# Two steps of a token mixer moved: the additions of a dilated attention block ahead of its filler, and the rounding of stick-breaking weights to another engine

## The chip, the cores and the metric

One core of a Trainium2 chip runs the kernel. The metric is the device time of one execution, in microseconds (us). Of the kernel before there are three timed runs: 1128.93, 1130.28 and 1131.22 us, with the median at 1130.28 us. The profile is of one further execution.

## What is computed

One decoder layer over 512 tokens of width 1024, in float32: a half-step SwiGLU FFN, a token-mixing sub-layer, a second half-step FFN, and an RMSNorm. The mixer reads one normalised input through one projection and runs two attentions on it. The stick-breaking one has 8 heads:

```python
strict = s_pos < t_pos
log_not = jnp.where(strict, jax.nn.log_sigmoid(-z), 0.0)
between = lax.cumsum(log_not, axis=3, reverse=True) - log_not
a = jnp.where(strict, jnp.exp(jax.nn.log_sigmoid(z) + between), 0.0)
outs.append(jnp.einsum('bhqk,bhkd->bhqd', a.astype(vb.dtype), vb))
```

The dilated one has 4 slots of keys and values and three groups of queries; the softmax groups of one slot are mixed by their denominators. Both outputs are projected, gated by sigmoids of the input, added, and projected once more.

## The kernel before

**Arithmetic.** TensorE multiplies at float32r, a rounded form of float32. To keep the precision each operand is held as a rounded high part and the rest as a low part, and a product is three matmuls (`product`, lines 1209 to 1211). So every weight tile of 128 x 1024 that a DMA brings costs one rounding copy on ScalarE (`split_hi`, line 489) and one subtraction on VectorE (`split_lo`, line 791), and every activation tile is split in the same way. ScalarE makes most high parts, VectorE all low parts. The tile `spA_hi` is an exception: VectorE rounds it too.

**Order.** Every engine runs its own queue in program order, and semaphores hold it at each hand-over. In the mixer all three compute engines follow one hand-written list, `MIX_STEPS` (made by `mix_schedule`, lines 106 to 168). Its fillers are half units of the projection (`Ua`, `Ub`, or `Us` for a short unit): 12 matmuls on TensorE each, while `Ua` and `Us` also carry the split of the weight tile two units later on ScalarE and VectorE. The fillers stand between the steps of the attentions, so that TensorE has matmuls to do while ScalarE and VectorE work on a head or a block.

**Stick-breaking heads 0 to 7** (about 380 to 530 us). `scores` makes the logits in three parts (512, 256 and 512 columns); ScalarE takes abs, exp and ln (lines 692 to 696), VectorE adds the maximum and splits the result (1098 to 1105). `suffix` sums it on TensorE with triangular matrices (1416, 1417); ScalarE takes the exponential of the three parts into `ebuf` (702), VectorE rounds each part into `spA_hi` (1113) and subtracts for `spA_lo` (1115). `pv` multiplies them by the values (1217, 1219). Between these stand the fillers, the rotation of the rotary projections (four ScalarE copies, line 648, then VectorE lines 1075 and 1080, then the split 683 and 1085) and the split of the outputs (716 and 1126).

**Dilated blocks 0 to 15** (about 525 to 665 us). Block n is slot n // 4 and quarter n % 4 of the queries. `dscores` makes the logits in `pair_bank`; VectorE takes the row maximum (1140) and its negative (1142), ScalarE the exponential with its sum into `prob` (730). `dadd` is the part that the change moves: VectorE takes the reciprocal of the sum (1151) and makes two additions (1155), and ScalarE multiplies `prob` by the reciprocal (736). `dturn` transposes `prob` on TensorE (1456) and ScalarE copies the rounded result to `pT_hi` (744); `dlo` subtracts on VectorE for `pT_lo` (1163). The `dscores` of the next block waits for the exponential, since `pair_bank` is single. Each `fill` here adds one filler. Before, one block stands in the list as:

```python
fill(DL_FILL[n] - 1)
...
s.append(("dadd", (j, r)))
if n + 1 < len(blocks):
    s.append(("dscores", blocks[n + 1]))
fill(1)
...
s.append(("dturn", (j, r)))
s.append(("dlo", (j, r)))
```

In blocks 0 to 3 the fillers and the `fin` steps behind them still carry rotary projections, which put the rotation (648) and its split on ScalarE and VectorE within each block; later blocks have gates in their place.

Of the kernel before, what the change touches and what calls it, by code (L numbers as in the profile page):

```python
# [78 lines left out]
SB_WIDTH = (512, 256, 512)  # L79
SB_AT = (0, 512, 768)  # L80
# [28 lines left out]
def mix_schedule():  # L109


    s = []
    halves = [(half, u) for u in range(MIX, END)
              for half in (("Us",) if u >= GATE and (u - GATE) % 2 else ("Ua", "Ub"))]

    def fill(n):
        for _ in range(n):
            half, u = halves.pop(0)
            s.append((half, u))

            if MIX < u <= GATE and half == ("Ub" if MIX_ORDER[u - 1 - MIX][0] in ("rq", "rk") else "Ua"):
                s.append(("fin", u - 1))
            if half == "Ub" and u >= GATE:
                s.append(("gate", u))
            if half == "Us":
                s.append(("merge", u))

    fill(2)
    s.append(("norm", 1))
    fill(4)  # L130
    s.append(("scores", 0))
    for h in range(2 * SB_PAIRS):
        fill(SB_FILL[h][0])
        if h:
            s.append(("y", h - 1))
        s.append(("suffix", h))
        if h:
            s.append(("ysplit", h - 1))
        fill(SB_FILL[h][1])
        s.append(("scores", h + 1) if h + 1 < 2 * SB_PAIRS else ("dscores", (0, 0)))  # L140
        s.append(("pv", h))
    blocks = [(j, r) for j in range(2 * DL_PAIRS) for r in range(DIL)]
    for n, (j, r) in enumerate(blocks):
        fill(DL_FILL[n] - 1)
        if n == 0:
            s.append(("y", 2 * SB_PAIRS - 1))
        if n == 1:
            s.append(("ysplit", 2 * SB_PAIRS - 1))
        s.append(("dadd", (j, r)))
        if n + 1 < len(blocks):  # L150
            s.append(("dscores", blocks[n + 1]))
        fill(1)
        if r == 0 and j:
            s.append(("dpv", j - 1))
        s.append(("dturn", (j, r)))
        s.append(("dlo", (j, r)))
        if r == 0 and j:
            s.append(("dy", j - 1))
        if r == 1 and j:
            s.append(("dysplit", j - 1))  # L160
    fill(len(halves))
    s.append(("dpv", 2 * DL_PAIRS - 1))
    s.append(("dy", 2 * DL_PAIRS - 1))
    s.append(("dysplit", 2 * DL_PAIRS - 1))
    return s
# [22 lines left out]
def build(nc, A, out):  # L188
    F32, F32R, BF16 = mybir.dt.float32, mybir.dt.float32r, mybir.dt.bfloat16
    ALU, ACT, AX = mybir.AluOpType, mybir.ActivationFunctionType, mybir.AxisListType  # L190
    ctx = ExitStack()
    with ctx:
# [56 lines left out]
        with ExitStack() as mix:  # L249
# [5 lines left out]
            with ExitStack() as att:  # L255
                raw = sb("raw", [P, 2, SEQ], F32, att)
                with ExitStack() as s:
                    spA_hi = sb("spA_hi", [P, 1280], F32R, s)
                    spA_lo = sb("spA_lo", [P, 1280], F32R, s)
                    ebuf = sb("ebuf", [P, 1280], F32, s)  # L260
# [94 lines left out]
        a_done = sem("a_done")  # L355
# [127 lines left out]
        def _(act):  # L483
# [153 lines left out]
            for kind, w in MIX_STEPS:  # L637
# [59 lines left out]
                elif kind == "suffix":  # L697
                    if w == 2 * SB_PAIRS - 1:
                        act.preload_act_table_set("exp_and_others")
                    for b in range(3):  # L700
                        act.wait_ge(suffix_done, 3 * w + b + 1)
                        act.activation(ebuf[:, SB_AT[b]:SB_AT[b] + SB_WIDTH[b]], bank[b][:, 0:SB_WIDTH[b]],
                                       ACT.Exp).then_inc(a_done, 1)
                elif kind in ("y", "dy"):

                    rows, other = head_rows(w), head_rows(w + 1)
                    n = w + (2 * SB_PAIRS if kind == "dy" else 0)
                    act.wait_ge(pv_done, n + 1)
                    if n >= 2:
                        act.wait_ge(ys_done, n - 1)  # L710
                    act.activation(ysum[rows, :], bank[3][other, :], ACT.Copy).then_inc(y_cross_done, 1)
                elif kind in ("ysplit", "dysplit"):
                    rows = head_rows(w)
                    if kind == "ysplit":
                        act.wait_ge(y_whole, w + 1)
                        act.activation(ys_hi[rows, w // 2, :], ysum[rows, :], ACT.Copy).then_inc(ys_hi_done, 1)
                    else:

                        act.wait_ge(y_whole, 2 * SB_PAIRS + w + 1)
                        act.activation(yd_hi[rows, w // 2, :].rearrange("c (p r) -> c r p", r=DIL),  # L720
                                       ysum[rows, :].rearrange("c (r p) -> c r p", r=DIL),
                                       ACT.Copy).then_inc(ys_hi_done, 1)
                elif kind == "dscores":
                    n = DIL * w[0] + w[1]
                    act.wait_ge(max_step, 2 * (n + 1))
                    if n >= 2:
                        act.wait_ge(pt_turned, n - 1)
                    if n == 0:
                        act.wait_ge(pv_done, 2 * SB_PAIRS)
                    act.activation(prob[:, n % 2, :], pair_bank[:, 0:6 * P], ACT.Exp,  # L730
                                   bias=stats[:, n % 2, 1:2], scale=HD ** -0.5,
                                   accum_out=stats[:, n % 2, 2:3]).then_inc(p_done, 1)
                elif kind == "dadd":
                    n = DIL * w[0] + w[1]
                    act.wait_ge(p_step, 3 * n + 3)
                    act.activation(prob[:, n % 2, 0:SEQ], prob[:, n % 2, 0:SEQ], ACT.Copy,
                                   scale=stats[:, n % 2, 3:4]).then_inc(p_scaled, 1)
                elif kind == "dturn":
                    j, r = w
                    n = DIL * j + r  # L740
                    act.wait_ge(pt_turned, n + 1)
                    if r == 0 and j:
                        act.wait_ge(pv_done, 2 * SB_PAIRS + j)
                    act.activation(pT_hi[:, :, r * P:(r + 1) * P], bank[2].rearrange("p (b c) -> p b c", b=DIL),
                                   ACT.Copy).then_inc(pt_hi_done, 1)
# [39 lines left out]
        def _(dve):  # L785
# [250 lines left out]
            for kind, w in MIX_STEPS:  # L1036
# [70 lines left out]
                elif kind == "suffix":  # L1107
                    for b in range(3):
                        t = 3 * w + b
                        cols = slice(SB_AT[b], SB_AT[b] + SB_WIDTH[b])  # L1110
                        dve.wait_ge(a_done, t + 1)
                        dve.wait_ge(suffix_done, 3 * w + 3)
                        dve.tensor_copy(spA_hi[:, cols], ebuf[:, cols]).then_inc(a_hi_done, 1)
                        dve.wait_ge(a_hi_done, t + 1)
                        dve.tensor_tensor(spA_lo[:, cols], ebuf[:, cols], spA_hi[:, cols].bitcast(F32),
                                          ALU.subtract).then_inc(a_split, 1)
# [450 lines left out]
```

## Time and profile before

| | |
|---|---|
| median of the three runs | 1130.28 us |
| profiled execution, its own time | 1132.13 us |
| its span | 1130.3 us |
| TensorE busy | 1106.8 us (98%) |
| VectorE busy | 769.8 us (68%) |
| ScalarE busy | 543.2 us (48%) |
| mean granted TensorE clock | 0.992 |

The profiled execution's own time is 1.8 us over its span and 1.9 us over the median of the runs. The profile names engines PE (TensorE), DVE (VectorE), ACT (ScalarE), POOL (GpSimd) and SP (the DMA queue). A timeline row gives the start and the duration in us, the engine, the line, the operation with its output and inputs, and in brackets the idle time of the engine before it with what ended it. An instruction may start before the one ahead of it has ended, by some tenths of a us; a row's `x4` stands for four instructions in a row.

### The profile page before, as it was taken

To read this page: it belongs to the slowest core of one execution; us is meant where nothing else is said; L and a number is where in the kernel's file an instruction comes from. 1 tells how busy PE (TensorE), PEld (TensorE's weight loads), DVE (VectorE), ACT (ScalarE), POOL (GpSimd) and SP (SyncE) were. 2 spreads that over 40 slices of the span, in tenths; PEclk is the share of its full clock that TensorE was granted. 3 is DMA by queue.
4 is the path that set the end of the run, shared out by engine and by line. 5 is a ranking of instruction groups with operands and counts; after the bars stand their busy time and mean duration, and the time that the engine had idled before them with its cause. 6 is when DMAs were issued, how large, how long until landed. Compare 5 with 4: busy or idle time off the path is not lost.

```text
span 1130.3 us, 15634 instructions
## 1 busy us (share of the span) xinstructions
PE 1106.8 (98%) x6057; PEld 948.1 (84%) x6065; DVE 769.8 (68%) x1074; ACT 543.2 (48%) x870; POOL 2.7 (0%) x6
## 2 busy tenths in 40 slices
PE   8999999999999999999999999999999999999996
PEld 6888899988998788877777778788898899889985
DVE  6876378745878778678765556667774588637863
ACT  6554155533653456567654443425452355415541
POOL 0000000000000000000000000000000000000000
PEclk9999999999999999999999999999999999999997
DMA  8223233333324212111121113422233323323222
GB/s 288 94 75 112 74 113 112 113 93 93 103 71 126 75 39 75 57 56 47 38 67 65 52 54 97 143 93 94 96 103 101 104 84 112 96 92 112 93 57 75
DMA packets 34440, 102.99 MB, mean 91 GB/s; under 512 B 4160, under 2 KB 7616, under 8 KB 34368
## 3 DMA queue, kind: packets, MB, share of 16 engines
q1 hardware_dynamic: 34368, 102.01, 28.3%
q8 instruction: 47, 0.77, 0.3%
q14 instruction: 25, 0.20, 0.1%
HBM read 99.90 MB, written 2.10 MB: 90 GB/s over the span
## 4 chain that ended last, share of the span: by engine, by line
PE 88%; DVE 4%; ACT 3%; issue 2%; SPq 1%; DMA 1%; POOL 0%; POOLq 0%; DVEq 0%; ACTq 0%
PE acc_pair L1209 25%; PE acc_pair L1211 25%; PE acc_pair L1210 25%; PE pair_bank L1209 2%; PE pair_bank L1211 2%; PE pair_bank L1210 2%; PE bank L1209 1%; PE bank L1211 1%; PE bank L1210 1%; ACT rope L648 1%; DVE w_lo L791 1%; ACT w_hi L489 1%; PE bank L1217 1%; PE bank L1219 1%; DMA w_raw<-in_w13a 1%
## 5 line engine op out<-in xcount | busy, mean ns | idle before, releaser
L1209 PE MATMUL acc_pair<-xg_hi,w_hi 128*128 128x512 f32 (+1 forms) x693 | 265.8, 384 | 1.7 <-DVE w_lo L1022 1.7
L1210 PE MATMUL acc_pair<-xg_lo,w_hi 128*128 128x512 f32 (+1 forms) x693 | 260.2, 375 | 0.0
L1211 PE MATMUL acc_pair<-xg_hi,w_lo 128*128 128x512 f32 (+1 forms) x693 | 259.4, 374 | 0.0
L489 ACT ACTIVATE w_hi<-w_raw 128x1024 fp32r<-128x1024 f32 (+3 forms) x159 | 154.4, 976 | 147.6 <-PE acc_pair L1211 147.3
L791 DVE TENSOR_TENSOR w_lo<-w_raw,w_hi 128x1024 fp32r<-128x1024 f32 (+3 forms) x159 | 178.6, 1126 | 42.9 <-ACT w_hi L489 37.5
L1211 PEld LDWEIGHTS acc_pair<-xg_hi,w_lo 128*128 128x128 f32 x693 | 130.7, 189 | 24.5
L1209 PEld LDWEIGHTS acc_pair<-xg_hi,w_hi 128*128 128x128 f32 x693 | 131.1, 189 | 23.9 <-issue 2.9
L1210 PEld LDWEIGHTS acc_pair<-xg_lo,w_hi 128*128 128x128 f32 x693 | 131.3, 189 | 20.3 <-issue 1.0
L1211 PE MATMUL acc_pair<-hid_hi,w_lo 128*128 128x512 f32 x352 | 138.8, 394 | 0.0
L1210 PE MATMUL acc_pair<-hid_lo,w_hi 128*128 128x512 f32 x352 | 138.2, 393 | 0.0
L1209 PE MATMUL acc_pair<-hid_hi,w_hi 128*128 128x512 f32 x352 | 136.9, 389 | 0.0
L962 DVE SCALAR_TENSOR_TENSOR x<-acc_pair,x 128x512 f32<-128x512 f32 x56 | 38.7, 691 | 113.8 <-PE acc_pair L1211 113.6
L1210 PEld LDWEIGHTS acc_pair<-hid_lo,w_hi 128*128 128x128 f32 x352 | 66.1, 188 | 15.0
L1209 PEld LDWEIGHTS acc_pair<-hid_hi,w_hi 128*128 128x128 f32 x352 | 66.1, 188 | 14.5
L1211 PEld LDWEIGHTS acc_pair<-hid_hi,w_lo 128*128 128x128 f32 x352 | 66.2, 188 | 13.4
L521 ACT ACTIVATE s_hi<-s_raw 128x1536 fp32r<-128x1536 f32 x35 | 52.1, 1488 | 47.5 <-DVE s_raw L863 47.5
L878 DVE TENSOR_TENSOR s_lo<-s_raw,s_hi 128x1536 fp32r<-128x1536 f32 x35 | 61.5, 1758 | 13.7 <-ACT s_hi L521 13.7
L890 DVE TENSOR_TENSOR acc_pair<-acc_pair,ysum 128x512 f32<-128x512 f32 x35 | 24.5, 700 | 56.1 <-PE acc_pair L1211 56.1
L1209 PE MATMUL acc_pair<-t_hi,s_hi 128*128 128x256 f32 x210 | 59.5, 283 | 2.6 <-ACT acc_pair L573 2.6
L1211 PE MATMUL acc_pair<-t_hi,s_lo 128*128 128x256 f32 x210 | 59.4, 283 | 0.0
L1210 PE MATMUL acc_pair<-t_lo,s_hi 128*128 128x256 f32 x210 | 59.3, 282 | 0.0
L536 ACT ACTIVATE gate<-gate 128x512 f32<-128x512 f32 x44 | 27.6, 627 | 49.6 <-DVE gate L892 49.6
(223 smaller groups left out, 2072.7 us busy)
## 6 DMA issues: line engine op xcount, KB each, us to landing
w_raw<-in_w13b SPq DMA_DIRECT2D x44, 512.0 KB, 3.6
w_raw<-in_w13a SPq DMA_DIRECT2D x40, 512.0 KB, 3.6
w_raw<-in_wmix SPq DMA_DIRECT2D x22, 512.0 KB, 3.5
w_raw<-in_w2a SPq DMA_DIRECT2D x16, 512.0 KB, 3.5
w_raw<-in_w2b SPq DMA_DIRECT2D x16, 512.0 KB, 3.6
w_raw<-in_wgate SPq DMA_DIRECT2D x8, 512.0 KB, 3.5
w_raw<-in_wend SPq DMA_DIRECT2D x8, 512.0 KB, 3.4
w_raw<-in_wo SPq DMA_DIRECT2D x8, 512.0 KB, 3.4
```

Source lines behind the costliest of these rows:

```text
L489: act.activation(w_hi[:, s, 0:width], w_raw[:, s, 0:width], ACT.Copy).then_inc(whi_done, 1)
L521: act.activation(s_hi[:, g % 2], s_raw[:], ACT.Copy).then_inc(s_hi_done, 1)
L536: act.activation(gate[:, f % 2, :], gate[:, f % 2, :], ACT.Silu).then_inc(silu_done, 1)
L648: act.activation(rope2[to:to + HD // 2, t % 2, :].rearrange("c (r p) -> c r p", r=DIL), acc[w % RING][c:c + HD // 2, :].rearrange("c (p r) ...
L791: dve.tensor_tensor(w_lo[:, s, 0:width], w_raw[:, s, 0:width], w_hi[:, s, 0:width].bitcast(F32), ALU.subtract).then_inc(wlo_done, 1)
L878: dve.tensor_tensor(s_lo[:, g % 2], s_raw[:], s_hi[:, g % 2].bitcast(F32), ALU.subtract).then_inc(s_lo_done, 1)
L890: dve.tensor_tensor(late, late, p5, ALU.add).then_inc(p5_added, 1)
L962: dve.scalar_tensor_tensor(x[:, m, :], acc[s][:], scale, x[:, m, :], ALU.mult, ALU.add).then_inc(acc_read[s], 1)
L1209: pe.matmul(o, w_h, r_h, start=first, stop=False, skip_group_check=check)
L1210: pe.matmul(o, w_h, r_l, start=False, stop=False, skip_group_check=check)
L1211: return pe.matmul(o, w_l, r_h, start=False, stop=last, skip_group_check=check)
L1217: pe.matmul(bank[3][:, col:SEQ], v[:, P * a:P * (a + 1)], a_h, start=first, stop=False, skip_group_check=True)
```

## The change

Two edits. The step `dadd` of every block moves ahead of the first filler of the block. And the three roundings of `ebuf` into `spA_hi` of each head leave VectorE; ScalarE does them behind the three exponentials, as activations with the function Copy, and VectorE's subtractions wait for them. VectorE's wait for the exponentials goes, since the copies stand behind those.

```diff
     for n, (j, r) in enumerate(blocks):
+        s.append(("dadd", (j, r)))
         fill(DL_FILL[n] - 1)
         if n == 0:
             s.append(("y", 2 * SB_PAIRS - 1))
         if n == 1:
             s.append(("ysplit", 2 * SB_PAIRS - 1))
-        s.append(("dadd", (j, r)))
         if n + 1 < len(blocks):
             s.append(("dscores", blocks[n + 1]))
         fill(1)
@@ scalar, kind == "suffix"
                         act.activation(ebuf[:, SB_AT[b]:SB_AT[b] + SB_WIDTH[b]], bank[b][:, 0:SB_WIDTH[b]],
                                        ACT.Exp).then_inc(a_done, 1)
+                    for b in range(3):
+                        cols = slice(SB_AT[b], SB_AT[b] + SB_WIDTH[b])
+                        act.wait_ge(a_done, 3 * w + b + 1)
+                        act.activation(spA_hi[:, cols], ebuf[:, cols], ACT.Copy).then_inc(a_hi_done, 1)
@@ vector, kind == "suffix"
                         cols = slice(SB_AT[b], SB_AT[b] + SB_WIDTH[b])
-                        dve.wait_ge(a_done, t + 1)
                         dve.wait_ge(suffix_done, 3 * w + 3)
-                        dve.tensor_copy(spA_hi[:, cols], ebuf[:, cols]).then_inc(a_hi_done, 1)
                         dve.wait_ge(a_hi_done, t + 1)
                         dve.tensor_tensor(spA_lo[:, cols], ebuf[:, cols], spA_hi[:, cols].bitcast(F32),
                                           ALU.subtract).then_inc(a_split, 1)
```

Lines of the changed kernel behind the edits are 4 higher on ScalarE and on VectorE up to the removed ones, and 2 higher after them. TensorE's order is the same in both.

ScalarE's queue at the `suffix` and `ysplit` steps of a head, up to the next weight split; before:

```order
L702 ACTIVATE ebuf<-pair_bank 128x512
L702 ACTIVATE ebuf<-pair_bank 128x256
L702 ACTIVATE ebuf<-bank 128x512
L716 ACTIVATE ys_hi<-ysum 64x512
L489 ACTIVATE w_hi<-w_raw 128x1024
```

and with the change:

```order
L702 ACTIVATE ebuf<-pair_bank 128x512
L702 ACTIVATE ebuf<-pair_bank 128x256
L702 ACTIVATE ebuf<-bank 128x512
L707 ACTIVATE spA_hi<-ebuf 128x512
L707 ACTIVATE spA_hi<-ebuf 128x256
L707 ACTIVATE spA_hi<-ebuf 128x512
L720 ACTIVATE ys_hi<-ysum 64x512
L489 ACTIVATE w_hi<-w_raw 128x1024
```

Three copies into `spA_hi` stand between the last exponential (702) and the split of the output, `ys_hi`, and the next weight split, `w_hi`.

VectorE's queue from `dlo` of block 1 to the row maximum of block 3; before:

```order
L1163 TENSOR_TENSOR pT_lo<-bank,pT_hi 128x4x128
L791 TENSOR_TENSOR w_lo<-w_raw,w_hi 128x1024
L1151 RECIPROCAL stats<-stats 128x1
L1155 TENSOR_TENSOR prob<-prob 128x128 x2
L1140 TENSOR_REDUCE stats<-pair_bank 128x1
```

and with the change:

```order
L1165 TENSOR_TENSOR pT_lo<-bank,pT_hi 128x4x128
L1153 RECIPROCAL stats<-stats 128x1
L1157 TENSOR_TENSOR prob<-prob 128x128 x2
L795 TENSOR_TENSOR w_lo<-w_raw,w_hi 128x1024
L1142 TENSOR_REDUCE stats<-pair_bank 128x1
```

The reciprocal and the additions for block 2 stand ahead of the weight split `w_lo` now, directly behind `pT_lo` of block 1.

ScalarE's queue at the same place, from the exponential of block 2 (L730, with the change L734) to that of block 3; before:

```order
L730 ACTIVATE prob,stats<-pair_bank,stats 128x768
L648 ACTIVATE rope<-acc_pair 32x512 x4
L683 ACTIVATE dq_hi<-roped 128x512
L744 ACTIVATE pT_hi<-bank 128x4x128
L489 ACTIVATE w_hi<-w_raw 128x1024
L736 ACTIVATE prob<-prob,stats 128x512
L730 ACTIVATE prob,stats<-pair_bank,stats 128x768
```

and with the change:

```order
L734 ACTIVATE prob,stats<-pair_bank,stats 128x768
L648 ACTIVATE rope<-acc_pair 32x512 x4
L683 ACTIVATE dq_hi<-roped 128x512
L748 ACTIVATE pT_hi<-bank 128x4x128
L740 ACTIVATE prob<-prob,stats 128x512
L489 ACTIVATE w_hi<-w_raw 128x1024
L734 ACTIVATE prob,stats<-pair_bank,stats 128x768
```

The scaling of block 2 (`prob<-prob,stats`) stands ahead of the weight split `w_hi` now, behind `pT_hi` of block 1.

## Rows read from the trace of the kernel before

**Rows 1.** The page: the span, and the busy time of the engines.

```profile
span 1130.3 us, 15634 instructions
...
PE 1106.8 (98%) x6057; PEld 948.1 (84%) x6065; DVE 769.8 (68%) x1074; ACT 543.2 (48%) x870; POOL 2.7 (0%) x6
```

**Rows 2.** Waits of TensorE: who released it, us in total, times, longest.

```profile
PE bank L1456 <- ACT prob L736: 1.6, 2, 1.1
...
PE pair_bank L1416 <- DVE spA_lo L1105: 1.4, 1, 1.4
...
PE bank L1217 <- DVE sv L1089: 0.5, 1, 0.5
```

**Rows 3.** Timeline of VectorE, 455 to 520: start, duration, operation.

```profile
473.41 0.43 DVE L1113 CAST spA_hi<-ebuf 128x512 fp32r<-128x512 f32 x1
...
475.59 0.69 DVE L1115 TENSOR_TENSOR spA_lo<-ebuf,spA_hi 128x512 fp32r<-128x512 f32 x1
...
491.12 0.41 DVE L1113 CAST spA_hi<-ebuf 128x512 fp32r<-128x512 f32 x1
...
493.30 0.69 DVE L1115 TENSOR_TENSOR spA_lo<-ebuf,spA_hi 128x512 fp32r<-128x512 f32 x1
```

**Rows 4.** Timeline of ScalarE, 455 to 530.

```profile
472.79 0.61 ACT L702 ACTIVATE ebuf<-bank 128x512 f32<-128x512 f32 x1
...
485.48 0.61 ACT L683 ACTIVATE sq_hi<-raw 128x512 fp32r<-128x512 f32 x1
...
490.94 0.60 ACT L702 ACTIVATE ebuf<-bank 128x512 f32<-128x512 f32 x1
...
527.48 2.43 ACT L648 ACTIVATE rope<-acc_pair 32x512 f32<-32x512 f32 x4 [2.88 <-DVE raw L1002]
```

**Rows 5.** Timeline of VectorE, 516 to 572.

```profile
550.39 0.68 DVE L1163 TENSOR_TENSOR pT_lo<-bank,pT_hi 128x512 fp32r<-128x512 f32 x1
...
551.28 1.23 DVE L791 TENSOR_TENSOR w_lo<-w_raw,w_hi 128x1024 fp32r<-128x1024 f32 x1 [0.21 <-ACT w_hi L489]
...
552.49 0.60 DVE L1155 TENSOR_TENSOR prob<-prob 128x128 f32<-128x128 f32 x2
...
553.01 0.95 DVE L1140 TENSOR_REDUCE stats<-pair_bank 128x1 f32<-128x768 f32 x1
```

**Rows 6.** Timeline of ScalarE, 516 to 572.

```profile
540.24 0.60 ACT L744 ACTIVATE pT_hi<-bank 128x512 fp32r<-128x512 f32 x1
...
545.57 0.90 ACT L730 ACTIVATE prob<-pair_bank,stats 128x768 f32<-128x768 f32 x1 [0.34 <-DVE stats L1142]
...
546.59 2.43 ACT L648 ACTIVATE rope<-acc_pair 32x512 f32<-32x512 f32 x4
...
549.70 0.60 ACT L744 ACTIVATE pT_hi<-bank 128x512 fp32r<-128x512 f32 x1
...
550.19 1.05 ACT L489 ACTIVATE w_hi<-w_raw 128x1024 fp32r<-128x1024 f32 x1
...
553.13 0.72 ACT L736 ACTIVATE prob<-prob,stats 128x512 f32<-128x512 f32 x1 [1.88 <-DVE prob L1155]
...
554.18 0.90 ACT L730 ACTIVATE prob<-pair_bank,stats 128x768 f32<-128x768 f32 x1 [0.33 <-DVE stats L1142]
...
558.31 0.60 ACT L744 ACTIVATE pT_hi<-bank 128x512 fp32r<-128x512 f32 x1
```

**Rows 7.** Timeline of TensorE, 540 to 575.

```profile
545.29 0.66 PE L1456 MATMUL bank<-identf,prob 128*128 128x128 f32 x4 [1.08 <-ACT prob L736]
...
548.64 0.50 PE L1209 MATMUL pair_bank<-dk_hi,dq_hi 64*128 64x512 f32 x1
...
553.90 0.66 PE L1456 MATMUL bank<-identf,prob 128*128 128x128 f32 x4 [0.47 <-ACT prob L736]
...
557.26 0.49 PE L1209 MATMUL pair_bank<-dk_hi,dq_hi 64*128 64x512 f32 x1
...
561.84 0.60 PE L1456 MATMUL bank<-identf,prob 128*128 128x128 f32 x4
```

## Prediction

> **What bounds the kernel now.** I read the page first: TensorE is busy for 1106.8 of the 1130.3 us of the span [rows 1], so only the remaining 23.5 us can be won by moving work between the other engines, and most of those lie at the start and the end of the program, which the change does not touch. Then I read the waits of TensorE. In the part that is touched they come to little: 1.6 us in two waits of a transposition (line 1456) for the scaling of `prob`, 1.4 us in one wait of the sums (1416) for `spA_lo`, and 0.5 us before one product with the values (1217) [rows 2]. So both edits together can win at most some 3.5 us. What they can lose is not bounded that way. So I read the timelines of VectorE and ScalarE around these waits, to see how late the two run behind TensorE and what sets their pace.
>
> **Edit 1, the rounding of the weights.** It takes 24 casts from VectorE: 16 of 512 columns at 0.41 to 0.43 us [rows 3] and 8 of 256 columns, shorter ones. It gives ScalarE 24 copies. A rounding copy of 512 columns from SBUF takes 0.61 us there [rows 4], and the next instruction can start some 0.1 us before it ends (`pT_hi` from 549.70 for 0.60 us, the next from 550.19 [rows 6]). What counts is when the last subtraction of a head ends, since behind it VectorE goes on to the work that TensorE will ask for.
>
> In head 4 VectorE casts first at 473.41 and starts its last subtraction at 475.59 [rows 3]. The last exponential on ScalarE starts at 472.79 [rows 4]. With the change the three copies start behind it at about 473.3, 473.8 and 474.15, and the last ends at 474.8; the three subtractions follow each copy by 0.04 us, and the last one starts at about 474.9, so 0.65 us sooner. In head 5 VectorE casts from 491.12 and subtracts last at 493.30 [rows 3]. There the last exponential starts at 490.94 [rows 4], pulled forward by the 0.65 us of head 4; the same count gives a last subtraction at 492.25, 1.05 us sooner. In head 6 the gain is small, because the weight split on ScalarE now stands behind three copies, and in head 7 it is nothing. With what is handed on through VectorE's unbroken queue, the first rotation ahead of the dilated blocks, at 527.48 [rows 4], comes 1.2 us sooner. For TensorE I take 1.1 us of the 1.4 us wait and a quarter of a us of the 0.5 us wait [rows 2]: 1.35 us, as long as nothing later takes it back. For heads 0 to 3 TensorE has no wait for this work; the copies' 1.5 us of ScalarE are hidden there by its idle times, and I put them at zero (if that cover were gone, 0.4 us in head 3, where ScalarE is busiest). Bounds for this edit: from 0 to 1.9 us sooner.
>
> The Trainium skill, "ScalarE: Activation LUTs", section "Rules for kernel authors", asks for a budget of about 0.3 us per activation and 0.83 ns per element. By that a copy of 512 columns would be estimated at 0.72 us, the trace has 0.61 us [rows 4], and three copies in a row would take about 0.6 us more per head than I count; over heads 4 and 5 the relief would be gone. What that makes of the time is the first rival.
>
> **Edit 2, the additions ahead of the filler.** TensorE waits for the scaling of blocks 1 and 2, 1.08 us and 0.47 us [rows 7]. The edit puts the additions, and ScalarE's scaling, ahead of the weight split of the filler. This brings the scaling forward, but by more waiting between the engines, and everything behind it comes later. Block 2 of before: `pT_hi` of block 1 starts on ScalarE at 549.70, the weight split `w_hi` follows at 550.19 [rows 6] while VectorE makes `pT_lo` (550.39), then `w_lo` at 551.28, the additions at 552.49 and the row maximum of block 3 at 553.01 [rows 5]. That is 3.3 us from `pT_hi` to the maximum.
>
> With the change the same work is a chain: `pT_lo` ends 1.4 us after the start of `pT_hi`; additions 0.60 us [rows 5], to 2.0 us; scaling 0.72 us [rows 6], of which 0.1 us overlaps with the next, to 2.65; `w_hi` 1.05 us, to 3.7; `w_lo` 1.23 us, and the maximum at about 4.9 us. So the maximum, and with it the exponential (554.18 before [rows 6]), the rotation of 2.43 us, the split and `pT_hi` of the next block come 1.6 us later per block. This is a closed loop: from one `pT_hi` to the next it took 8.61 us (549.70 to 558.31) [rows 6], more than TensorE's own 7.94 us from 553.90 to 561.84 [rows 7]. It was the loop, not TensorE, that set the pace of blocks 1 and 2. It becomes 10.2 us.
>
> I follow `pT_hi` of block 2, at 558.31 before [rows 6]. It comes 1.2 us sooner by edit 1; 0.25 us later by block 0, where most of the added chain is absorbed by a wait that was there; 1.4 us later by block 1 (540.24 to 549.70, 9.46 us before [rows 6], 10.85 now); 1.6 us later by block 2. That puts it at 560.35. The scaling of block 3 ends 2.75 us behind it, at 563.1, and TensorE's transposition of block 3, at 561.84 before without a wait [rows 7], starts at 563.15: 1.3 us later.
>
> The waits show the same. The 1.08 us of block 1 go. But `dscores` of block 3, which ran at 548.64, needs the exponential that started at 545.57, and `dscores` of block 4 (557.26) the one that started at 554.18 [rows 6, 7]; each now waits about 0.85 us. The transpositions of blocks 2 and 3 wait about 1.1 and 1.3 us. From block 3 on the rotation leaves the loop. ScalarE and VectorE are 4 to 6 us later than before by then and win it back over blocks 4 to 7, during which TensorE reaches them with under 0.5 us to spare; for this I add 0.45 us (none to 1). After that the shift stays as it is, since the rest of the program is TensorE's. DMA is no part of this: the weight splits are later by 2 to 5 us, while a tile is split about two units ahead of its use.
>
> **Sum.** 1.3 + 0.45 = 1.75 us later than the profiled execution, so 1133.9 us against its own 1132.13 us. That execution lies 1.9 us over the median; against the median of 1130.28 us the same shift gives **1132.0 us**. With 0 to 1.9 us for edit 1, 0.2 us per pass of the loop either way and the tail's bounds, this case runs from 1130.5 to 1133.5 us.
>
> **The rivals.**
>
> *No relief from edit 1* (chance 0.2). If the copies on ScalarE cost 0.7 us each and don't overlap, heads 4 and 5 end where they did. For it speaks that ScalarE holds back weight splits too, which VectorE then waits for; against it that a rounding copy takes 0.61 us [rows 4] and that the next one overlaps with it [rows 6]. Then the 1.2 us are missing from the loop's start: 2.95 us later, 1133.2 us, from 1132.5 to 1134.5 us.
>
> *Faster* (chance 0.13). The mechanism is slack in the loop of blocks 1 and 2: if the scaling runs in ScalarE's idle 1.88 us [rows 6] and the weight split still reaches the row maximum in time, the two waits of 1.55 us [rows 7] go and the 1.35 us of the heads stay, together 2.9 us, 1127.4 us; with half of it 1128.8 us. It decides from the point at which the maximum comes less than 0.5 us later per block; I count 1.6 us. Against it speaks that every step of the new chain has an instruction that waits for the one before it.
>
> *They cancel* (chance 0.17). The relief of the heads and the waits of the blocks come out equal, because block 1 absorbs more than I count, or TensorE's arrival at block 3 has some slack: 1129.8 to 1130.8 us, at 1130.3 us.
>
> **How the numbers follow.** The forecast has a chance of 0.5. A measurement of this kernel tells a difference of about 0.2%, 2.26 us, from none. Of the forecast's range only the upper part is slower by more than that, a third of it (0.17), and of the first rival nearly all (0.2): 0.37. Of the faster case about half passes the bound: 0.07. The rest, 0.56, is within 0.2%. The range from 1129.0 to 1134.3 us takes in the forecast, most of the first rival and the upper part of the faster one.
>
> **What would show it right or wrong.** In the changed kernel's waits of TensorE: no wait of the transposition of block 1; new waits of line 1209 into `pair_bank` for the exponential (line 734), about 0.85 us each, at `dscores` of blocks 3 and 4; waits of 1.1 and 1.3 us for the scaling (740) at blocks 2 and 3; the wait for `spA_lo` down from 1.4 to 0.3 us. In ScalarE's timeline: 24 copies of line 707 at about 0.6 us for the wide ones, and 10.2 us between `pT_hi` of blocks 1 and 2. It would be wrong if that distance stays under 9.2 us, if the copies take over 0.7 us, or if waits appear in the later blocks, which I count as TensorE's.

## The result, and the profile after

The changed kernel takes 1135.80 us (median of six runs, 1132.80 to 1137.44), and the kernel before 1130.62 us (six runs, 1128.93 to 1131.22). The ratio is 1.0045 with an interval of 1.0031 to 1.0060. So it is slower by 5.2 us, where 1.75 us was forecast, and lies outside the range of 1129.0 to 1134.3 us. The sign of the sum was right. Its size was not.

The page of the changed kernel, in the same two places as [rows 1]; this execution's own time is 1137.42 us:

```profile
span 1135.6 us, 15634 instructions
...
PE 1109.8 (98%) x6057; PEld 949.9 (84%) x6065; DVE 760.3 (67%) x1050; ACT 552.8 (49%) x894; POOL 2.7 (0%) x6
```

VectorE gave up 9.5 us of work and ScalarE took 9.6 us on. That moves no bound: TensorE is busy for 98% as before, and its own busy time is 3.0 us longer, although it has the same matmuls. This last number is worth a stop: a wait leaves the matmuls behind it almost as they were (four transpositions take 0.66 us behind a wait and 0.60 us without one, [rows 7]), so a few waits don't make 3 us of busy time. It will come back as the clock.

The waits of TensorE from 380 to 680 us in the changed kernel (engine, tile and line, what ended the wait: us in total, times, longest), against [rows 2]:

```profile
PE pair_bank L1211 <- ACT prob L734: 2.3, 2, 1.4
PE bank L1458 <- ACT prob L740: 2.0, 2, 1.0
PE bank L1219 <- issue: 1.9, 1, 1.9
...
PE pair_bank L1418 <- DVE spA_lo L1109: 0.6, 1, 0.6
PE bank L1219 <- DVE sv L1093: 0.4, 1, 0.4
```

Two waits of `dscores` for an exponential (first line) are new, 2.3 us. The transpositions still wait twice, now 2.0 us for 1.6. The wait for `spA_lo` fell from 1.4 to 0.6 us. The third line is the product of the last block with `dv`; before it was 1.5 us, in a group that the prediction did not use (`issue` stands where the profile shows nothing that ended the wait):

```profile
PE bank L1217 <- issue: 1.5, 1, 1.5
```

Where the new waits lie is seen in TensorE's timeline (start, duration, and in brackets the idle time before). These are `dscores` of block 3, the transposition of block 2, `dscores` of block 4 and the transposition of block 3; that of block 1 starts at 544.65 without a wait.

```profile
549.36 0.46 PE L1211 MATMUL pair_bank<-dk_hi,dq_hi 64*128 64x512 f32 x1 [1.35 <-ACT prob L734]
...
555.11 0.66 PE L1458 MATMUL bank<-identf,prob 128*128 128x128 f32 x4 [1.02 <-ACT prob L740]
...
559.49 0.46 PE L1211 MATMUL pair_bank<-dk_hi,dq_hi 64*128 64x512 f32 x1 [0.97 <-ACT prob L734]
...
565.24 0.33 PE L1458 MATMUL bank<-identf,prob 128*128 128x128 f32 x1 [0.99 <-ACT prob L740]
```

ScalarE's timeline through two passes of the loop, to be laid beside [rows 6]:

```profile
541.36 0.60 ACT L748 ACTIVATE pT_hi<-bank 128x512 fp32r<-128x512 f32 x1
...
552.34 0.60 ACT L748 ACTIVATE pT_hi<-bank 128x512 fp32r<-128x512 f32 x1
554.34 0.72 ACT L740 ACTIVATE prob<-prob,stats 128x512 f32<-128x512 f32 x1 [1.39 <-DVE prob L1157]
554.96 1.04 ACT L489 ACTIVATE w_hi<-w_raw 128x1024 fp32r<-128x1024 f32 x1
558.35 0.90 ACT L734 ACTIVATE prob<-pair_bank,stats 128x768 f32<-128x768 f32 x1 [2.35 <-DVE stats L1144]
...
562.47 0.60 ACT L748 ACTIVATE pT_hi<-bank 128x512 fp32r<-128x512 f32 x1
```

and VectorE's in the same pass, beside [rows 5]:

```profile
553.03 0.68 DVE L1165 TENSOR_TENSOR pT_lo<-bank,pT_hi 128x512 fp32r<-128x512 f32 x1
...
553.70 0.60 DVE L1157 TENSOR_TENSOR prob<-prob 128x128 f32<-128x128 f32 x2
556.04 1.23 DVE L795 TENSOR_TENSOR w_lo<-w_raw,w_hi 128x1024 fp32r<-128x1024 f32 x1 [1.74 <-ACT w_hi L489]
557.18 0.95 DVE L1142 TENSOR_REDUCE stats<-pair_bank 128x1 f32<-128x768 f32 x1
```

Read the brackets as a relay. ScalarE stands 1.39 us for the additions, and has not yet made `w_hi`. VectorE then stands 1.74 us for `w_hi`, and so the row maximum starts 4.84 us behind `pT_hi` (557.18 less 552.34), where it was 3.31 us. Each engine idles in turn for the other. From `pT_hi` of block 1 to that of block 2 it takes 10.13 us for 8.61 us.

**The account of the two profiled executions.** I set marks at TensorE's starts that both traces have, and compare the distance between them:

| stretch | before | after | difference |
|---|---|---|---|
| scores of head 1 to values product of head 6 | 114.89 | 114.05 | -0.84 |
| values product of head 6 to `dscores` of block 0 | 10.11 | 11.61 | +1.50 |
| `dscores` of block 0 to the transposition of block 3 | 36.23 | 39.02 | +2.79 |
| transposition of block 3 to the last block's product | 100.81 | 101.49 | +0.68 |
| last block's product to the start of the projection behind the mixer | 56.95 | 58.55 | +1.6 |

These make +5.7 us of the span's +5.3; the rest of the program is 0.4 us shorter. The first, third and fourth rows are waits, +2.6 us together. The second and fifth are none. There TensorE's clock is lower. (Of the fourth, 0.2 us is no wait either: it falls in the few matmuls right behind the first mark.) Its windows in the changed kernel (stretch, length, busy time and instructions, granted clock, DMA share, GB/s):

```profile
510.00:515.00 5.00, 4.58 (x23) 0.95 0.08 7
515.00:520.00 5.00, 5.00 (x20) 0.71 0.26 97
...
665.00:670.00 5.00, 3.27 (x11) 0.81 0.09 26
670.00:675.00 5.00, 5.00 (x20) 0.85 0.00 0
```

### The profile page after: what moved, and what is told of

It is laid out like the page before. It is cut to its first block, busy times and chain, and to the rows that moved or that the text cites. A ratio compares the mean times of both kernels' runs of the same rounds, so it can differ in the third digit from the quotient of the medians.

```text
span 1135.6 us, 15634 instructions
## 1 busy us (share of the span) xinstructions
PE 1109.8 (98%) x6057; PEld 949.9 (84%) x6065; DVE 760.3 (67%) x1050; ACT 552.8 (49%) x894; POOL 2.7 (0%) x6
## 4 chain that ended last, share of the span: by engine, by line
PE 86%; DVE 5%; ACT 4%; issue 3%; SPq 1%; DMA 1%; POOL 0%; POOLq 0%; DVEq 0%; ACTq 0%
PE acc_pair L1211 24%; PE acc_pair L1212 24%; PE acc_pair L1213 24%; PE pair_bank L1211 2%; PE pair_bank L1213 2%; PE pair_bank L1212 2%; ACT rope L648 1%; PE bank L1211 1%; PE bank L1213 1%; PE bank L1212 1%; ACT w_hi L489 1%; PE bank L1219 1%; PE bank L1221 1%; DVE w_lo L795 1%; DMA w_raw<-in_w13a 1%
```

## The experiments

Two theories were set against each other. **The loop** (L): the change lengthens the closed loop of blocks 0 to 3, and what it costs is the waits shown. **The clock** (C): part of the loss comes from stretches at the lower of TensorE's two levels, which the loop doesn't explain. Each experiment has a profiled trace, from which the same marks are read, and timed runs beside the kernel before. The numbers of all stand in one table behind the last of them.

**One edit at a time.** The additions alone:

```diff
     for n, (j, r) in enumerate(blocks):
+        s.append(("dadd", (j, r)))
         fill(DL_FILL[n] - 1)
...
-        s.append(("dadd", (j, r)))
```

> Edit 2 alone: the additions and the scaling ahead of the first filler in all blocks; VectorE keeps rounding the weights. Theory L (the loop): the time is lost because the scaling stands ahead of the weight split on ScalarE, which makes the loop from one pT_hi to the next 10.1 us in blocks 1 and 2 (8.6 us before). In the changed kernel's trace the rotation ahead of block 0 was 0.70 us later than before and the transposition of block 3 3.40 us later, so blocks 0 to 3 cost 2.7 us; with 0.2 us in the blocks behind and 0.5 us at the last product, L expects 3.4 us more than before, new waits for the exponential (line 730) of 0.9 to 1.4 us at dscores of blocks 3 and 4, and full clock from 500 to 530 us. Rival C (the clock): the blocks cost nothing net, and what was lost is TensorE at its lower clock after waits, some 1.5 us in each such stretch; C expects under 1 us more than before where no such stretch shows, and 1.5 us for each that does.

Measured: 1134.66 us, ratio 1.0044 (1.0031 to 1.0057). Blocks 0 to 3 take 38.95 us, +2.72 against before, as in the changed kernel, and the waits are the same ones:

```profile
PE pair_bank L1209 <- ACT prob L730: 2.2, 2, 1.3
PE bank L1456 <- ACT prob L736: 2.0, 2, 1.0
PE bank L1217 <- issue: 2.0, 1, 2.0
PE pair_bank L1416 <- DVE spA_lo L1105: 1.4, 1, 1.4
```

The loss belongs to this edit. The wait for `spA_lo` stays at 1.4 us, as it must without the other.

The rounding alone (the diff is the scalar and vector part of the change, and no part of the list):

> Edit 1 alone: ScalarE rounds the weights, the additions stay behind the filler. Both theories take the relief of the heads from the changed kernel's trace: the product at 515.50 us before starts 0.9 us sooner. L expects 0.9 us less than before if the clock stays up, with the loop of blocks 1 and 2 at 8.6 us and the waits for the scaling as before. C expects a stretch of the lower clock from 514.6 to 517.6 us again, which belongs to this edit, and so 0.6 us more than before, with the loop at 8.6 us.

Measured: 1130.34 us, ratio 0.9993 (0.9981 to 1.0005), not to be told from before. By the marks the heads are 0.87 us shorter, and blocks 0 to 3 take 36.21 us, unchanged. So the relief is there, but it is under a us, and nothing takes it back.

**Which blocks.** The additions ahead of the filler in blocks 4 to 15 only:

```diff
     for n, (j, r) in enumerate(blocks):
+        if n >= 4:
+            s.append(("dadd", (j, r)))
         fill(DL_FILL[n] - 1)
...
-        s.append(("dadd", (j, r)))
+        if n < 4:
+            s.append(("dadd", (j, r)))
```

> Both edits, but the additions stand ahead of the filler only in blocks 4 to 15, whose fillers carry no rotation; blocks 0 to 3 have them behind it as before. L expects the loss of 2.7 us in blocks 0 to 3 to be gone, the loop of blocks 1 and 2 at 8.6 us, no new wait for the exponential, and at most 0.5 us left at the last product: 0.4 us less than before at full clock. If instead the blocks from 4 on carry a cost of their own, it shows here as waits after 570 us and more than 1 us over before.

Measured: 1133.83 us, 1.0035 (1.0022 to 1.0048), in five runs. The trace says the opposite of the time: blocks 0 to 3 are back at 36.23 us and only the last product waits longer (1.9 us for 1.5), so at the same clock this kernel would be 0.37 us faster than before. Its profiled run indeed took 1129.82 us; the four others took 1133.7 to 1135.0 us, at granted clocks that average lower. This is the first sign of lost time that no wait shows, and it was not what the loop theory wants. The clock is the candidate, no more. It was run again:

> e3 again, unaltered: its first trace is 0.4 us faster than before between the marks, its timed runs are slower by a ratio of 1.0035 with a mean granted clock of 0.992 against 0.9945 of before. If that was a matter of the executions drawn, the ratio falls to about 0.9997 with a mean clock near 0.9945. If the order of the late blocks brings the clock down, the ratio stays above 1.002 and the mean clock below 0.993, and this trace shows where.

Measured: 1132.53 us, 1.0010 (0.9999 to 1.0021), twelve runs, mean 1131.97 us, with the same marks. A milder result than the first, on the same side, but its interval doesn't exclude that nothing changed.

The additions ahead in blocks 0 to 3 only (the same diff, with `n < 4` and `n >= 4` exchanged):

> Both edits, with the additions ahead of the filler in blocks 0 to 3 only, the counterpart of e3. L expects the whole 2.8 us of blocks 0 to 3 here, new waits for the exponential at dscores of blocks 3 and 4, 0.85 us less in the heads, and the last product's wait at 1.5 us: 2.1 us over before at full clock. If the loss came from the many late blocks, it is within 0.5 us of before.

Measured: 1134.08 us, 1.0032 (1.0018 to 1.0047). Blocks 0 to 3 take 39.04 us, and the last product waits 1.5 us as before. The whole loss of 2.8 us in waits of the blocks needs only these four.

And the late blocks without the rounding on ScalarE:

> The additions ahead of the filler in blocks 4 to 15 alone, without edit 1: heads and blocks 0 to 3 as before, at most 0.5 us more at the last product. At full clock 0.5 us over before. If the late blocks bring the clock down, it is 2 us or more over before with a mean clock below 0.993; if not, between 0 and 1 us over.

Measured: 1132.65 us, 1.0024 (1.0010 to 1.0039), while the marks give only +0.5 us. The late blocks thus come with lost time that no wait in the traces shows, with either placing of the rounding.

**The scaling left where it was.** If the loop is long because ScalarE stands for the additions ahead of its weight split, then VectorE's additions can go ahead while ScalarE's scaling stays behind. The list gets a step of its own for the scaling:

```diff
     for n, (j, r) in enumerate(blocks):
+        s.append(("dadd", (j, r)))
         fill(DL_FILL[n] - 1)
...
-        s.append(("dadd", (j, r)))
+        s.append(("dscale", (j, r)))
...
-                elif kind == "dadd":
+                elif kind == "dscale":
```

The last two lines are in ScalarE's function; the rounding is on ScalarE as in the change.

> Both edits, with edit 2 only on VectorE: the reciprocal and the additions stand ahead of the first filler, while ScalarE's scaling stays behind the weight split of the filler, where it was. By L the loss comes from the scaling in front of the weight split: here the split runs beside pT_lo and the additions again, and from pT_hi to the row maximum I count 0.6 us for pT_hi to its copy's end, 0.7 pT_lo, 0.6 additions and 1.2 w_lo, 3.1 us against 3.3 us before and 4.9 us with the change. So the loop is about 8.4 us, the scaling is ready 1.3 us sooner than before, and the waits of 1.08 and 0.47 us go: 1.5 to 2.5 us less than before at full clock. If the cost lies in the additions on VectorE themselves, this kernel is as slow as the changed one, 3 us or more over before.

Measured: 1129.38 us, 0.9992 (0.9979 to 1.0004). Blocks 0 to 3 take 34.86 us: 1.37 us less than before, 4.16 us less than with the change. Of the four waits of the change one is left:

```profile
PE bank L1459 <- ACT prob L741: 0.2, 1, 0.2
```

ScalarE's timeline of this kernel, block 2:

```profile
547.64 0.60 ACT L749 ACTIVATE pT_hi<-bank 128x512 fp32r<-128x512 f32 x1
548.14 1.05 ACT L490 ACTIVATE w_hi<-w_raw 128x1024 fp32r<-128x1024 f32 x1
549.63 0.72 ACT L741 ACTIVATE prob<-prob,stats 128x512 f32<-128x512 f32 x1 [0.44 <-DVE prob L1158]
551.83 0.90 ACT L735 ACTIVATE prob<-pair_bank,stats 128x768 f32<-128x768 f32 x1 [1.47 <-DVE stats L1145]
```

and VectorE's:

```profile
549.00 0.60 DVE L1158 TENSOR_TENSOR prob<-prob 128x128 f32<-128x128 f32 x2
549.52 1.22 DVE L796 TENSOR_TENSOR w_lo<-w_raw,w_hi 128x1024 fp32r<-128x1024 f32 x1
550.65 0.95 DVE L1143 TENSOR_REDUCE stats<-pair_bank 128x1 f32<-128x768 f32 x1
```

`w_hi` now runs beside `pT_lo` and the additions. VectorE finds it ready and stands nowhere, and the maximum starts 3.01 us behind `pT_hi`. The scaling, which is what TensorE waits for, starts 1.99 us behind `pT_hi`, where it was 3.43 us before [rows 6] and 2.00 us with the change. So the scaling comes as early as in the change, and the weight split doesn't pay for it.

The same order with the rounding left on VectorE:

> The order of e4 (additions ahead of the filler on VectorE, scaling behind the weight split on ScalarE) without edit 1. L expects blocks 0 to 3 to take 1.4 us less than before, as in e4, since the loop is shorter whatever the rounding, and the heads to take as long as before: 1.3 us less than before at full clock, against 2.1 us less for e4. If the gain of e4 came only from its earlier start into the blocks, this kernel shows under 0.5 us.

Measured: 1129.90 us, 0.9995 (0.9984 to 1.0006), blocks 0 to 3 in 34.85 us. The gain of the blocks doesn't need the other edit. In time it is not shown to be faster than before.

The first of the two once more, since it was the best:

> e4 again, unaltered, for a narrower interval: 2.1 us less than before at full clock (heads 0.85, blocks 0 to 3 1.4 us), which with the mean clock of its first runs (0.9936 against 0.9945) leaves about 1 us; a ratio of 0.998 to 0.9995.

Measured: 1128.09 us, twelve runs, 0.9979 (0.9966 to 0.9993). It beats before by about 2 us and the change by more than 6; the run before it left zero just inside its interval, so this is a small gain, clear of zero in one of two measurements.

**The wait of the last product.** In the changed kernel's trace the wait of 1.94 us before the last product is followed by a stretch at the lower level. Blocks 14 and 15 in the old order (`n < 14` ahead, `n >= 14` behind):

> Both edits, but in blocks 14 and 15 the additions stay behind the filler. TensorE's wait ahead of the last product, 1.94 us with the change and 1.46 us before, should be about 1.5 us again, which wins 0.4 us at full clock. The kernel with late blocks only (e3) is 0.4 us faster than before by its trace but 3.5 us slower in its timed runs. If the longer wait at the last product is what brings the lower clock at 668 us (C), this kernel is faster than the changed one by 0.4 us and up to 1.5 us more; if not, by 0.4 us alone, about 1135.4 us.

Measured: 1135.44 us, 1.0040 (1.0026 to 1.0055). The wait is back at 1.5 us and the time is no better. So taking the longer wait away did not win the time back. Whether it changes how often the clock falls, six executions can't tell: their mean clock is 0.9937, and that is uncertain by 0.001.

**The pair again**, to have the clock of more executions:

> The changed kernel again, unaltered, for a second trace. Between marks of the two traces, the changed kernel at full clock should cost 2.6 us more than before: 0.85 us less up to the product of head 6, 2.8 us more in blocks 0 to 3, 0.7 us more from there to the last product. By L these three parts repeat within 0.2 us in this trace. By C the stretches of the lower clock (385, 515 and 668 us in the first trace, about 1.5 us each) belong to the change and stand at the same places again; if they are a matter of the single execution, at least one of them is missing here, and the run is shorter by 1.5 us for each.

> The kernel before again, for a second trace: same marks within 0.2 us at full clock. In the first trace one stretch of the lower clock cost time (385 us). If such stretches fall by the single execution, this trace can have another number of them, at 385, 515 or 668 us, and the span moves by 1.5 us for each; if they belong to the kernel, only the one at 385 us shows.

Measured: the change 1134.68 us, 1.0042 (1.0027 to 1.0057), with marks as in its first trace (blocks 0 to 3 in 39.04 us) and neither of the two low stretches behind the heads. Before: 1130.24 us, 1.0003 (0.9990 to 1.0017).

**All of them, by waits and by clock.** The column "waits" is the difference from before in the marks' three waiting stretches, from one trace each, less what a low stretch adds where one falls into them (0.9 us in the trace of the last kernel, the only such case). The column "clock at most" is what a lower mean clock would take if TensorE had work in every us of the span: 1133 us times the difference of the mean granted clocks, where 83 executions of before have 0.9943 (mean time 1130.56 us). It is an upper bound, as is shown below the table.

| kernel | runs | waits, us | mean clock | clock at most, us | sum | mean time less before |
|---|---|---|---|---|---|---|
| before again | 10 | 0.0 | 0.9951 | -1.0 | -1.0 | -0.4 |
| change | 6 | +2.6 | 0.9927 | +1.8 | +4.4 | +5.1 |
| change again | 8 | +2.6 | 0.9925 | +2.0 | +4.6 | +4.4 |
| additions alone | 5 | +3.5 | 0.9940 | +0.3 | +3.8 | +4.5 |
| rounding alone | 12 | -0.9 | 0.9949 | -0.8 | -1.6 | -0.6 |
| late blocks | 5 | -0.4 | 0.9918 | +2.8 | +2.4 | +2.9 |
| late blocks again | 12 | -0.4 | 0.9928 | +1.7 | +1.3 | +1.4 |
| late blocks, rounding on VectorE | 12 | +0.5 | 0.9927 | +1.8 | +2.3 | +2.8 |
| early blocks | 12 | +2.2 | 0.9931 | +1.3 | +3.5 | +3.8 |
| last two blocks behind | 6 | +2.3 | 0.9937 | +0.7 | +3.0 | +4.5 |
| scaling behind | 11 | -2.1 | 0.9936 | +0.7 | -1.4 | -1.1 |
| scaling behind again | 12 | -2.1 | 0.9945 | -0.3 | -2.4 | -1.9 |
| scaling behind, rounding on VectorE | 12 | -1.3 | 0.9952 | -1.1 | -2.4 | -0.5 |

The mean times are uncertain by 0.4 to 0.9 us each. With that, ten of the twelve sums of changed kernels meet the time within 1.1 us; the kernel with the last two blocks behind misses by 1.5 and the last row by 1.9 us. Against the 25 executions of before that ran beside these two (0.9950, 1130.24 us) they miss by 1.0 and 1.5 us. But eleven of the twelve sums are too small, so something of about half a us is in none of the columns.

The clock's price in the table is too high, and the executions say by how much. Among the 83 of before, all of one kernel, the time rises by 0.63 us (standard error 0.04) for each 0.001 of mean clock, and within the sets of the other kernels by 0.74 us; the table takes 1.13 us. The trace of before shows why. TensorE's clock is low from 1118.60 us to the end in it, and that is more than half of the whole shortfall (5.9 of 9.3 us), but there TensorE has little to run and then nothing:

```profile
1110.00:1118.00 8.00, 7.34 (x39) 1.00 0.00 1
1118.00:1124.00 6.00, 4.41 (x22) 0.55 0.16 58
1124.00:1130.00 6.00, 0.00 (x0) 0.50 0.78 291
```

At 0.63 us the clock takes 1.1 us of the change (0.9926 over its fourteen executions), not 1.9 us, and then all twelve sums are too small, by 0.3 to 1.8 us.

## Why the prediction was wrong in size

**The loop, foreseen and there.** The distance between two `pT_hi` was put at 10.2 us; it is 10.13 us. From `pT_hi` of block 0 to that of block 1 it was put at 10.85 us; it is 10.98 us (541.36 to 552.34). The maximum was put at about 4.9 us behind `pT_hi`; it is 4.84 us. The prediction had `dscores` of block 0 start 1.35 us sooner and the transposition of block 3 start 1.3 us later, so the stretch between was 2.65 us longer; measured it is 2.79 us. So the mechanism was right, and two slips in it are small: block 0 adds 0.4 us behind the first rotation where 0.25 us was said, and block 1 adds 1.5 us where 1.4 us was said. No wait is left at block 1, as said. The single waits are distributed otherwise: 1.35 and 0.97 us at `dscores` of blocks 3 and 4 (0.85 each was said), 1.02 and 0.99 us at the transpositions of blocks 2 and 3 (1.1 and 1.3 said).

**First step that failed: the relief of the heads, 1.35 us.** VectorE's part came as counted in head 4 and nearly in head 5: the last subtraction ends at 475.62 us for 476.28 before (0.66 us sooner, 0.65 said) and at 493.13 for 493.99 (0.86, where 1.05 was said). The rows, of the copies of head 4 on ScalarE and of the subtractions of head 4 on VectorE:

```profile
473.24 1.47 ACT L707 ACTIVATE spA_hi<-ebuf 128x512 fp32r<-128x512 f32 x3
```

```profile
473.99 1.63 DVE L1117 TENSOR_TENSOR spA_lo<-ebuf,spA_hi 128x512 fp32r<-128x512 f32 x3 [0.63 <-ACT spA_hi L707]
```

Three copies, of 512, 256 and 512 columns, take 1.47 us together, so the overlap on which the sum rested is there. The budget of the Trainium skill, "ScalarE: Activation LUTs", section "Rules for kernel authors", would estimate about 2 us for the three (0.5 us over the prediction's 1.5 us, not the 0.6 us that it says), but it is stated for an activation with its bias as a pointer operand, and the copies name no bias. The trace decides: 1.47 us. The 1.05 us is a slip of the prediction's own count. It has the last subtraction of head 4 start 2.1 us behind the last exponential (474.9 less 472.79); "the same count" from an exponential at 490.29 gives 492.4, so 0.9 us sooner, and not 492.25. And TensorE got just what VectorE gained in head 5: the wait for `spA_lo` fell by 0.84 us, not by 1.1, and the wait for `sv` by 0.07 us, not by a quarter. By the marks it is 0.84 us in all in this trace and 0.87 us in that of the rounding alone. Nothing built up further through VectorE's queue: where 1.2 us was said for the first rotation, the second traces of the pair show 0.7 us, counted from the scores of head 1. Cost of the error: 0.5 us.

**Second: the tail, 0.45 us.** It measured 0.68 us. About 0.2 us of it falls in the first 4 us behind the transposition of block 3; the other half us is at a place that I had counted as TensorE's alone. Before, the last low part started as soon as ScalarE's `pT_hi` had come. VectorE's rows before, and then with the change:

```profile
660.43 0.43 DVE L791 TENSOR_TENSOR w_lo<-w_raw,w_hi 128x256 fp32r<-128x256 f32 x1 [1.13 <-ACT w_hi L489]
660.79 0.69 DVE L1056 SCALAR_TENSOR_TENSOR gsb_tiles<-gsb_tiles,acc_pair 128x512 f32<-128x512 f32 x1
661.86 0.69 DVE L1163 TENSOR_TENSOR pT_lo<-bank,pT_hi 128x512 fp32r<-128x512 f32 x1 [0.38 <-ACT pT_hi L744]
```

```profile
665.00 0.42 DVE L795 TENSOR_TENSOR w_lo<-w_raw,w_hi 128x256 fp32r<-128x256 f32 x1 [1.11 <-ACT w_hi L489]
665.34 0.68 DVE L1060 SCALAR_TENSOR_TENSOR gsb_tiles<-gsb_tiles,acc_pair 128x512 f32<-128x512 f32 x1
665.94 0.68 DVE L1165 TENSOR_TENSOR pT_lo<-bank,pT_hi 128x512 fp32r<-128x512 f32 x1
```

Now the low part of a weight tile, `w_lo`, comes late in front of it: it starts 0.8 us behind TensorE's transposition at 664.19, where it started 0.2 us ahead of the one at 660.59. The merge of the gates follows it without a gap, and `pT_lo` has no slack left. It is the relay again: ScalarE stands 1.99 us for the additions of the last block, and the gates' activation and `w_hi` stand behind its scaling. The experiments with the old order in the last blocks have 1.5 us there, those with the new one 1.9. The prediction said that waits in the later blocks would prove it wrong, and this is one.

**Third, and the largest: time that is in no wait, of which TensorE's clock is a part.** The waits alone give 2.6 us, which would have been 1132.9 us, inside the range. The mean of the change's fourteen executions is 4.7 us over before, so about 2 us more is neither a wait nor another instruction. The prediction added up waits and took TensorE's own pace as given, a term put at nothing without a reason, although it had the clock of 0.992 in front of it. The mean clock is 0.9926 over both sets of the change against 0.9943, and that difference of 0.0017 (standard error 0.0006) is clear of noise. It is worth 1.1 us at the price that the executions of before show, and 1.9 us at most. What the remaining 0.2 to 1 us is stays open. **Why** the mean clock is lower is open too, and so is whether it is the stretches within the mixer or the one at the end of the program: the eight traces with the additions and the scaling ahead in some block have eight low stretches between 380 and 700 us, the six others five. The late blocks with the additions ahead have the low mean with either rounding (0.9918, 0.9928, 0.9927), although they add only half a us of wait. With one trace per kernel I can't locate the stretches of the timed runs.

**The rivals.** "No relief from edit 1" is refuted by the rounding alone: 0.87 us of relief, though its time of 1133.2 us was nearest. "Faster" fell with the loop, which is 1.5 us longer per pass where under 0.5 us was needed. "They cancel" fell too: block 1 absorbed less than was counted, and the marks have 3.5 us of loss against 0.84 us of relief.

## What to carry to other kernels

When a step of a shared list is moved, look at it once for each engine that takes part: the half that hands over may go forward while the half that waits stays behind work that is ready to run, and here the difference between the two was 4.2 us. When two engines in program order hand work to and fro, count the distance from one pass to the next, not the instructions; that number came out within 0.15 us. And where TensorE is busy for 98% of the time, a change under half a per cent can't be forecast from waits alone: give the clock a term, or at least a bound, take the clock of many executions before a difference is explained, and take its price from executions of one kernel, since a mean over the span counts low clock too where TensorE has nothing to run.

## What the runs showed of the hardware

**The clock falls for some 3 us behind short waits, in some executions.** In the changed kernel's trace TensorE waits 0.42 us for `sv` at head 6 and then runs at half rate. Two rows of it, and the same two of the kernel with the additions in the late blocks, after a wait of 0.41 us:

```profile
514.61 0.79 PE L1219 MATMUL bank<-spA_hi,sv 128*128 128x512 f32 x1 [0.42 <-DVE sv L1093]
515.20 0.63 PE L1221 MATMUL bank<-spA_lo,sv 128*64 128x512 f32 x1
```

```profile
512.67 0.49 PE L1222 MATMUL bank<-spA_hi,sv 128*128 128x512 f32 x1 [0.41 <-DVE sv L1096]
513.00 0.40 PE L1224 MATMUL bank<-spA_lo,sv 128*64 128x512 f32 x1
```

Up to this point both kernels have the same instructions in the same order on every engine. The windows of the second have a granted clock of 1.00 throughout here:

```profile
510.00:515.00 5.00, 4.59 (x26) 1.00 0.35 105
515.00:520.00 5.00, 5.00 (x34) 1.00 0.00 0
```

Within the first, the granted clock is 0.50 from 515 to 517 us, which is the level of 1.2 GHz, and 2.4 GHz again from 518 us. From the values product of head 6 to `dscores` of block 0 it takes 11.61 us in the one and 10.12 us in the other. The same is seen at about 385 us (18.79 us instead of 17.21 from the scores of head 0 to those of head 1) and behind the last product (58.55 instead of 56.95): 1.5 to 1.6 us each time. One stretch cost less: in the kernel with the scaling behind and the rounding on VectorE it begins at 502.75 us and adds 0.9 us, and TensorE waits no more for `sv` a few us later. Of the nine traces in which head 6 is made by the changed code up to this place, three have the stretch at about 515 us and six don't. A wait comes up to 3 us ahead of each of them, from 0.42 us to 1.94 us long, but the same wait is followed by full clock in other executions. So that the wait brings it about is not shown. A stretch in the first 30 us costs nothing that the marks show. All fourteen traces end at the lower level, for the last 3 to 12 us of the span.

**A single trace says little about a difference of 2 us.** The change's two traces have spans of 1135.6 and 1132.4 us with the same waits. The first trace alone would have put 3.1 us down to the two low stretches; over fourteen executions the mean clock leaves 1.1 to 1.9 us.
